# Gathering the tokens of two experts at once, as a rounded part and a remainder, in the mixture-of-experts stage of a two-block transformer kernel

## What is computed

```python
def moe_swiglu(h, router, w_gate, w_up, w_down):
    t = h.reshape(b * s, d)                       # 256 x 1024
    logits = (t @ router).astype(jnp.float32)     # 256 x 8
    top_val, top_idx = lax.top_k(logits, TOP_K)   # 2 of 8
    top_w = jax.nn.softmax(top_val, axis=-1)
    gates = jnp.sum(jax.nn.one_hot(top_idx, N_EXPERTS) * top_w[..., None], axis=1)
    out = jnp.zeros_like(t)
    for e in range(N_EXPERTS):
        out = out + gates[:, e:e + 1] * swiglu_2(t, w_gate[e], w_up[e], w_down[e])
    return out.reshape(b, s, d)                   # hidden width of an expert: 2816
```

## Time and profile before

| | us |
|---|---|
| median of 3 runs | 2635.41 |
| lowest and highest | 2633.11, 2635.43 |
| the profiled execution | 2635.67 |
| its span, first to last instruction | 2633.9 |
| PE busy | 2396.4 (91%) |
| DVE busy | 1770.4 (67%) |
| ACT busy | 1320.5 (50%) |
| mixture-of-experts stage, from its first pick matrix on | about 838 |

### The profile page before, as it was taken

How to read it: one execution, slowest core, us unless ns; L and a number is a source line. 1 busy time by engine, 2 the same in 40 slices (tenths; PEclk the granted TensorE clock), 3 DMA queues, 4 the chain that set the end, 5 groups by cost and what they waited for, 6 DMA issues and landing times. The chain is left out here.

```text
span 2633.9 us, 44570 instructions
## 1 busy us (share of the span) xinstructions
PE 2396.4 (91%) x17195; PEld 2175.7 (83%) x17195; DVE 1770.4 (67%) x2860; ACT 1320.5 (50%) x2068; POOL 186.5 (7%) x171
## 2 busy tenths in 40 slices
PE   7898999889988989979789987488999999999998
PEld 5787898679878779979689987377999999999997
DVE  3555555555555555565755556657999999999997
ACT  2343433433443534442444432135778777777776
POOL 0500000000005000008100012100000000000000
PEclk9899999989998989989799987778999999999999
DMA  8524555155633044534045541025999999999995
GB/s 342 196 96 176 192 216 201 64 208 216 234 131 139 6 176 173 188 124 160 1 155 183 190 182 49 0 89 209 343 340 342 334 342 338 336 344 332 337 346 214
DMA packets 82228, 542.86 MB, mean 206 GB/s; under 512 B 9328, under 2 KB 9840, under 8 KB 33904
## 3 DMA queue, kind: packets, MB, share of 16 engines
q1 hardware_dynamic: 79184, 529.57, 54.3%
q10 hardware_dynamic: 2848, 10.55, 1.1%
HBM read 539.03 MB, written 1.05 MB: 205 GB/s over the span
## 5 line engine op out<-in xcount | busy, mean ns | idle before, releaser
L847 PE MATMUL bank<-w_hi,src_hi 128*128 128x256 f32 x2304 | 664.0, 288 | 16.2 <-DVE src_lo L618 6.7
L3017 DVE TENSOR_TENSOR w_lo<-ring,w_hi 128x1024 fp32r<-128x1024 f32 x528 | 637.3, 1223 | 46.1 <-ACT w_hi L2946 33.7
L848 PE MATMUL bank<-w_lo,src_hi 128*128 128x256 f32 x2304 | 656.4, 285 | 0.0
L849 PE MATMUL bank<-w_hi,src_lo 128*128 128x256 f32 x2304 | 654.9, 284 | 0.0
L847 PEld LDWEIGHTS bank<-w_hi,src_hi 128*128 128x128 f32 x2304 | 444.8, 193 | 35.2 <-issue 25.0
L848 PEld LDWEIGHTS bank<-w_lo,src_hi 128*128 128x128 f32 x2304 | 445.3, 193 | 6.8
L849 PEld LDWEIGHTS bank<-w_hi,src_lo 128*128 128x128 f32 x2304 | 446.0, 194 | 0.0
L847 PE MATMUL bank<-src_hi,w_hi 128*128 128x256 f32 x1472 | 426.4, 290 | 13.1 <-DVE w_lo L1177 8.9
L1177 DVE TENSOR_TENSOR w_lo<-ring,w_hi 128x1024 fp32r<-128x1024 f32 x264 | 322.9, 1223 | 168.9 <-ACT w_hi L1114 168.8
L848 PE MATMUL bank<-src_lo,w_hi 128*128 128x256 f32 x1472 | 421.6, 286 | 0.0
L849 PE MATMUL bank<-src_hi,w_lo 128*128 128x256 f32 x1472 | 421.4, 286 | 0.0
(11 more groups left out here) (421 smaller groups left out, 2794.5 us busy)
## 6 DMA issues: line engine op xcount, KB each, us to landing
ring<-in_moe SPq DMA_DIRECT2D x176, 1024.0 KB, 7.2
ring<-in_ffn SPq DMA_DIRECT2D x66, 1536.0 KB, 6.6
ring<-in_moe SPq DMA_DIRECT2D x176, 512.0 KB, 6.8
ring<-in_ffn_ev SPq DMA_DIRECT2D x22, 1536.0 KB, 6.5
oT<-in_w_ada SPq DMA_DIRECT2D x20, 1024.0 KB, 5.5
big<-in_w_ada SPq DMA_DIRECT2D x20, 1024.0 KB, 8.3
ring<-in_w_in SPq DMA_DIRECT2D x18, 1024.0 KB, 6.4
ring<-in_w_out SPq DMA_DIRECT2D x12, 1024.0 KB, 4.9
```

Of the source, the lines that this page charges most:

```text
L847: pe.matmul(out, ah, bh, start=start and i == 0, stop=False, skip_group_check=True)
L848: pe.matmul(out, ah, bl, start=False, stop=False, skip_group_check=True)
L849: mm = pe.matmul(out, al, bh, start=False, stop=stop and i == n - 1, skip_group_check=True)
L3017: dve.tensor_tensor(wl, piece, wh.bitcast(F32), ALU.subtract).then_inc(p.w_lo[kind].sem, 1)
```

## The change

1. `route`: ACT rounds the gained `xn` into `xn_hi` (over `gates`), two Copies of 128x1024, and DVE subtracts it into `xn_lo` (over `ctx_res`), two subtractions of 128x1024. On DVE these stand between the expert weights and the wait for the counts. The loop's trip count becomes `most / 2 - 1` in place of `most - 3`.
2. `gather` fetches two experts at once: 8 feature tiles by 2 token halves by 2 (`xn_hi`, `xn_lo`), 32 float32r matmuls of 256 columns in place of twice 32 float32 matmuls of 128 columns. They come in four parts of 8 matmuls, in banks 5, 6, 7 and 5, at r = 12, 13, 14 and 17 of every odd job. Part 3 waits in addition for the remainder of part 0. `keep_job` and `keep_rest` have four parts of 128x512, at r = 15, 16, 17, 20 and 16, 17, 18, 21.
3. `make_pick` makes four comparisons at r = 6 of every odd job, in place of two in every job.
4. Sources alternate between two pairs of tiles (`src_hi`, `src_lo` and `src_hi2`, `src_lo2`); the latter, and `pick`, lie in space of `big` and `work` that is free by then.
5. `walk`: three jobs written out, four in the loop (1 to 3 times), one after it. With 8 jobs the loop runs once in both kernels.
6. Before `walk` four parts are gathered and split, not two.

```diff
+            act.wait_ge(*p.sig("gained")(1))
+            for t in range(NT):
+                act.activation(p.xnH[:, t, :], p.xn[:, t, :], ACT.Copy).then_inc(p.sig("xn_hi").sem, 1)
...
             chain(ins)
+            for t in range(NT):
+                dve.wait_ge(*p.sig("xn_hi")(t + 1))
+                ins = dve.tensor_tensor(p.xnL[:, t, :], p.xn[:, t, :], p.xnH[:, t, :].bitcast(F32), ALU.subtract)
+            chain(ins)
             dve.wait_ge(*counted(1))
...
-            chain(dve.tensor_scalar(most, most, -3.0, None, ALU.add))
+            chain(dve.tensor_scalar(most, most, 0.5, -1.0, ALU.mult, ALU.add))
...
+    GATHER_AT = (12, 13, 14, 17)
+    S_BANK, G_BANK = (6, 7, 5, 6), (5, 6, 7, 5)
+    sources = ((p.srcH, p.srcL), (p.srcH2, p.srcL2))
...
-        for b in range(NE - 3):
+        for b in range(NE - 5):
...
-            for b in (NE - 3, NE - 2):
+            for b in range(NE - 5, NE - 1):
...
-                pe.wait_ge(*job_at(picked, i, 1, j + 1))
-                for k in range(4 * part, 4 * part + 4):
+                pe.wait_ge(*job_at(picked, i, 1, j + 2))
+                if part == 3:
+                    pe.wait_ge(*job_at(job_lo, i, 2, 2 * j + 1))
+                for k in range(2 * part, 2 * part + 2):
                     for t in range(NT):
-                        mm = pe.matmul(p.ps[G_BANK[part]][:, (k % 4) * P:(k % 4) * P + P], xn[:, t, k * P:k * P + P],
-                                       pick[:, j % 2, t, :], start=t == 0, stop=t == NT - 1)
+                        for v in (p.xnH, p.xnL):
+                            mm = pe.matmul(p.ps[G_BANK[part]][:, (k % 2) * T:(k % 2) * T + T], v[:, t, k * P:k * P + P],
+                                           pick[:, j // 2 % 2, t, :], start=t == 0 and v is p.xnH,
+                                           stop=t == NT - 1 and v is p.xnL)
...
-                if 12 <= r < 14 and not last:
-                    if not first:
-                        pe.wait_ge(*job_at(added, i, 4, 4 * b))
-                    gather(i, b + 1, r - 12)
+                if r in GATHER_AT and b % 2 and not last:
+                    pe.wait_ge(*job_at(added, i, 4, 4 * b))
+                    gather(i, b + 1, GATHER_AT.index(r))
...
-                if 15 <= r < 17 and not last:
-                    keep_job(i, b + 1, r - 15)
+                if r - 3 in GATHER_AT and b % 2 and not last:
+                    keep_job(i, b + 1, GATHER_AT.index(r - 3))
...
-                if r == 6 and not last:
-                    if not first:
-                        dve.wait_ge(*job_at(wt_turned, i, 1, b))
+                if r == 6 and b % 2 and not last:
+                    dve.wait_ge(*job_at(wt_turned, i, 1, b))
                     make_pick(i, b + 1)
-                if 16 <= r < 18 and not last:
-                    keep_rest(i, b + 1, r - 16)
+                if r - 4 in GATHER_AT and b % 2 and not last:
+                    keep_rest(i, b + 1, GATHER_AT.index(r - 4))
```

More of the change, by code:

```diff
@@ L2752, in moe @@
     DOWN = 2
-    xn = p.xn
-    big, work = p.big, p.work
-    pick = big[:, 0:512].rearrange("p (b t s) -> p b t s", b=2, t=NT)
+    work = p.work
+    pick = p.pick
     WT, yH, yL = p.pickT[:], p.yH[:], p.yL[:]
@@ L2798, in walk @@
         for r in range(FC + 3):
-            step(between, NE - 3, r, False, True)
+            step(between, NE - 5, r, False, True)
     def there(r, lag, first):
@@ L2839, in turn_weights @@
                 for t in range(NT):
-                    mm = pe.transpose(p.ps[5][:, t * P:t * P + P], pick[:, j % 2, t, :], p.ident[:, :])
+                    mm = pe.transpose(p.ps[5][:, t * P:t * P + P], pick[:, j // 2 % 2, t, (j % 2) * P:(j % 2) * P + P].bitcast(F32),
+                                      p.ident[:, :])
                 mm.then_inc(wt_turned.sem, 1)
@@ L2911, in step @@
                         scatter(i, b, q)
-            pe.wait_ge(*p.sig("gained")(1))
-            gather(0, 0, 0)
-            gather(0, 0, 1)
+            for part in range(4):
+                gather(0, 0, part)
             walk(pe, between, step)
@@ L2971, in step @@
                     keep_output(i, b)
-            for part in range(2):
+            for part in range(4):
                 keep_job(0, 0, part)
@@ L2978, in _ @@
         def _(dve):
-            between = dve.value_load(p.trip[0:1, 1:2], min_val=1, max_val=5)
+            between = dve.value_load(p.trip[0:1, 1:2], min_val=1, max_val=3)
             iota = p.con_at(CON2, "iota")
             def make_pick(i, j):
[L2985 to L2988, removed]
+                for m in range(2):
+                    job = slice(j + m, j + m + 1) if isinstance(i, int) else bass.ds(i * 4 + (j + m), 1)
+                    for t in range(NT):
+                        ins = dve.tensor_scalar(pick[:, j // 2 % 2, t, m * P:m * P + P], iota, p.slot[:, t, job], None,
+                                                ALU.is_equal)
+                    ins.then_inc(picked.sem, 1)
             def keep_rest(i, j, part):
                 dve.wait_ge(*job_at(job_hi, i, 2, 2 * j + part + 1))
-                ks, ss = slice(4 * part, 4 * part + 4), slice((j % 2) * P, (j % 2) * P + P)
-                dve.tensor_tensor(p.srcL[:, ks, ss], p.ps[G_BANK[part]][:, :].rearrange("p (k s) -> p k s", k=4),
-                                  p.srcH[:, ks, ss].bitcast(F32), ALU.subtract).then_inc(job_lo.sem, 1)
+                high, low = [v[:, 2 * part:2 * part + 2, :].rearrange("p k s -> p (k s)") for v in sources[j // 2 % 2]]
+                dve.tensor_tensor(low, p.ps[G_BANK[part]][:, :], high.bitcast(F32), ALU.subtract).then_inc(job_lo.sem, 1)
             def add_scattered(i, j, q):
```

33 lines of the change are left out of this document (20 added, 13 removed).

## The result

The changed kernel took 2619.39 us (median of 5 runs, 2618.15 to 2622.43), against 2633.11 us (2630.47 to 2635.43) for the kernel before on the same chip: ratio 0.9949, 95% interval 0.9935 to 0.9964, or 13.7 us less. The saving itself did not leave it: counted from 2635.41 us, from which the forecast set out, the range stood for savings of 6.9 to 14.9 us, and 13.7 lies inside. In this comparison the kernel before was itself 2.3 us faster than 2635.41. The profiled execution of the changed kernel took 2618.65 us, with a span of 2616.9.

The account below looks back on a forecast made before the run. PE was taken to bound the kernel. From the profiled 2635.67 us, -25.0 + 11.3 + 0.2 + 1.2 + 0.4 + 0.4 = -11.5 us led to a forecast of 2624.0 us, range 2620.5 to 2628.5.

Parts of the forecast that it names:

- PE bounds the walk: Expert stage: PE, busy 791.5 of 797.0 us, sets the pace, so what is taken from it comes off the time.
- -25.0 + 11.3 + 0.2 = -13.5 for the walk: Walk: seven gathers removed (25.0 us), three pairs added (11.3), register wait values in two more jobs (+0.2).
- The count of the gather's matmuls: Old gather in the walk: taken as 32 float32 matmuls of 128 columns, 0.112 us each, 3.57 us a gather.
- the trace shows half of what four passes cost: Old float32 gather: four passes would be 0.213 us a matmul, 6.8 us a gather; the trace was read as half.
- loads not hidden: Gather: 190 ns weight loads stand in line with matmuls, 0.308 us each; slower, 2646 us; chance 0.04.
- 23 starts of the same shape: New gather's price: 23 float32r starts in existing chunks, 2.71 us, give 0.118 us a matmul, 3.77 us a pair.
- waiting for DVE: Walk: PE is not the bound and the saving turns into waiting; only additions count, 2638 us; chance 0.08.
- Routing +1.2 and +0.4: Before the walk: two DVE subtractions less idle time, +1.2 us; PE waiting for four comparisons, not two, +0.4 us.
- First gather +0.4: Before the walk: 32 matmuls all at the low clock, 6.8 us against 6.11, so +0 to +0.8, taken as +0.4.
- against it that it is at the low level by then in any case: Clock rival, walk's start: argument against 1.6 us more PE idling changing the slow stretch; rival 2621 to 2627 us, chance 0.06.
- The front as a whole: Routing, comparisons and first gather before the walk: additions of 1.2, 0.4 and 0.4 us, together +2.0.
- no such stretch: Walk's start, clock rival: first products escape the low clock, giving 2621 us; rival's chance 0.06.

Follow-up runs that it names:

- gather_twice: The kernel after with each gather part in the walk issued twice; walk 802.56 us, ratio 0.9992 to the kernel before.
- pair_f32: The kernel after without the split: pairs gathered in plain float32, 16 matmuls of 256 columns; ratio 0.9998 to the kernel before.
- single_f32r: The kernel before with xn_hi and xn_lo made in routing, one expert gathered at a time by 32 float32r matmuls of 128 columns; ratio 1.0014.
- fill_before: The kernel before plus the filler, seven unneeded 128-column float32 matmuls in the PE gap behind the first gather; ratio 1.0000, repeated 0.9998.

## Why the prediction was right in the walk and wrong in front

- **PE bounds the walk.** Right. `gather_twice` shows it with an edit: 11.2 us more for PE, 11.2 us more walk.
- **-25.0 + 11.3 + 0.2 = -13.5 for the walk.** Measured -13.48 (804.83 to 791.35). Its lower bound was added up wrongly, without effect: from 24.4 us removed it is 24.4 - 11.3 - 1.2 = 11.9, not 12.5. A pair costs 3.74 us where 3.77 was forecast. The even and odd jobs at 98.8 and 102.5, the gather's chunks at 5.3 and the eight stalls of 0.8 all came as foretold.
- **The count of the gather's matmuls was wrong**, there and in the description of the kernel before: a gather is 8 x 2 = 16 float32 matmuls (8 in each part), not 32. The trace lists each float32 matmul as two records: the seven matmuls of the filler stand above as x14. One takes 3.57 / 16 = 0.223 us. The prediction had said that the trace shows half of what four passes cost. That falls: the Trainium skill, "FP8 and Floating Point Precision", section "TensorE Precision Notes", gives four passes for float32. Four passes of 128 columns at 2.4 GHz are 0.213 us, an estimate, and this case's trace agrees with 0.223, as it does at 256 columns with 0.43, where the estimate is 0.427. For the same reason columns of both forms do not cost the same at the low level: a float32 matmul of 128 columns took two records of 0.22 us, a float32r one of 256 columns 0.21. The sum didn't suffer, since it took the gather's time in the walk from the length of chunks, and the first gather's from 32 matmuls of the new form.
- **Rival "loads not hidden".** Not so at 256 columns: 0.117 us and not 0.308. But a floor exists: with a fresh weight each, float32r matmuls of 64 and of 128 columns cost 0.113 us alike. At 256 columns this floor is just covered. The prediction's step, to take the price from 23 starts of the same shape, is what kept it right.
- **Rival "waiting for DVE".** Not so; 10.2 us of cover for two jobs, where 10.0 was forecast.
- **Routing +1.2 and +0.4.** Measured +1.52.
- **First gather +0.4.** Wrong sign: -0.59. The step took all of it at the low level; 2.3 us of it ran at the high one, since it begins later and the clock rose at the same place behind the start of routing.
- **The step that failed: "against it that it is at the low level by then in any case".** With this the prediction kept the slow stretch behind the gap as it was and gave a change of it, either way, 0.06. The stretch is gone in every profile of the kernel after, -2.44 us. The front as a whole was forecast at +2.0 and measured at +1.52 - 0.59 - 2.44 = -1.5. In the range "no such stretch" stood as 2621, by itself, while the clock's rise also shortens the first gather.

Put together: the profiles say -13.5 - 1.5 = -15.0 where -11.5 was forecast, which would have given 2635.67 - 15.0 = 2620.7, just inside the range. The 3.5 us between -11.5 and -15.0 are all in the front. From there to 2619.4 it is 1.3 us, less than the kernel before itself moves from one session to the next (medians 2633.0 to 2637.0), and the part ahead of routing, 2.27 us shorter in the first profile of the kernel after, can do that. So that the time fell out of the range took both: the front, and 1.3 us of chance.

What stays open. First, whether executions without the profiler have the slow stretch as the profiled ones do. Three comparisons of the two kernels gave 0.9949, 0.9943 and 0.9965; -11.5 us (0.9956) lies in all three intervals, -15.0 (0.9943) in two, and the fillers' 2.4 us can't be resolved. Second, what decides whether the clock holds over the gap of 2.98 us. A shorter gap held it in all five profiles that have one. With the whole gap it depends on more than the time at the high level (`pair_f32`), and on more than the form of the gather: `gather_twice` has the front of the kernel after, and there the clock rose later, at 19.8 us, the first gather took 9.48 us, and the clock fell. Nor does `single_f32r` with its 8.45 us rule out float32r as a cause, since its clock had not risen at all before the gap. Third, what sets the place of the rise: 17.9 us behind the start of routing in ten profiles, 19.6 to 30.1 in the other eight. No run here varied the first gather by itself.

## What to carry to other kernels

Cost an edit to the bounding engine by the distance between starts of the same shape in the same stage, and split a compound change in two before believing its parts: here either half alone was worth nothing, since a float32r matmul of 64 or 128 columns cost nearly as much as one of 256, and a float32 one of 128 columns twice that. Where an engine's clock rises and falls around the edited stretch, take both ends of it into the sum as cases with a real chance, together with what they do to the neighbouring stretches: an edit that only moves the start of the work moves how much of it lies ahead of the rise. Count instructions in the code, not in the trace's records.

## What the runs showed of the hardware

- A float32r matmul with a fresh 128x128 weight cost 0.113 us at 64 columns, 0.112 at 128 and 0.117 at 256. The Trainium skill, "TensorE: Matmul & The Clock Gate", section "Back-to-back issue gap", gives N / 2.4 + 2.5 ns, by which 256 columns would take 0.109, an estimate; no run here reached it. Its section "LDWEIGHTS (loading the stationary operand)" gives columns / 1.2 ns for a weight load, 0.107 us for 128, an estimate. The distance of 0.11 us between the starts of loads is near it; the profile's load records last 0.19 us each and overlap. The prediction hadn't set this rule beside the rival.
- A float32 matmul stands in the trace as two records, and so does its weight load (14 records of each for the seven matmuls of `fill_before`).
- Over a PE gap of 2.98 us the clock fell from its high level in six of eleven profiles in which it had risen, once after 4.0 us at the high level (`pair_f32`), and held in five, after 1.8 to 2.3 us. Over a gap of 1.42 us it held in five of five. The fall came inside the gap, in the three profiles of the kernel before 2.1 us after the gather's last matmul.
- While POOL ran a subtraction of 128x1024 (4.77 us for two), a DVE instruction on 128x2 took 2.38 us and one on 128x16 took 2.35, in place of 0.17. The Trainium skill, "SBUF — State Buffer", section "SBUF: two separate sides", says that a GpSimd instruction that reads SBUF and a DVE instruction with two SBUF inputs take a shared pair of ports as an exclusive lock, for a whole instruction at a time; the trace agrees: 2.38 us is half of 4.77.
